# Even heads of a hybrid decoder step: ScalarE's work ordered by function table, and the queries' sums of squares ahead of the keys' product

## The reference

```python
qkv = jax.nn.silu(causal_dwconv(concat([q, k, v]), conv_prev, conv_w))
q = l2norm(split_heads(q, DN_HEADS)) * (DN_HEAD_DIM ** -0.5)   # x * rsqrt(sum(x * x) + EPS)
k = l2norm(split_heads(k, DN_HEADS))
beta = jax.nn.sigmoid(b);  G = jnp.cumsum(g, axis=-1)
decay = jnp.exp(jnp.where(causal, G[..., :, None] - G[..., None, :], -jnp.inf))
a_mat = eye + einsum('bnhid,bnhjd->bnhij', k * beta, k) * decay * strict
u_base = triangular_solve(a_mat, v * beta)
w_mat = triangular_solve(a_mat, k * beta * exp(G))
aqk = einsum('bnhid,bnhjd->bnhij', q, k) * decay
# then a scan over the chunks with q, k, G, u_base, w_mat, aqk; o is normed and multiplied by silu(z)
```

## Time and profile before

| | |
|---|---|
| median of 3 runs | 1917.39 us |
| profiled execution | 1914.43 us |
| its span, first to last instruction | 1912.6 us |
| time outside the span | 1.83 us |
| mean granted clock of TensorE | 0.978 of full |
| PE busy | 1816.6 us, 95% of the span |
| ACT busy | 619.5 us, 32% |
| POOL busy | 849.4 us, 44% |
| DVE busy | 592.2 us, 31% |
| the four even heads | about 62 to 460 us of the span |

### The profile page before, as it was taken

How to read it: one execution, slowest core, us unless ns; L and a number is a source line. 1 busy time by engine, 2 the same in 40 slices (tenths; PEclk the granted TensorE clock), 3 DMA queues, 4 the chain that set the end, 5 groups by cost and what they waited for, 6 DMA issues and landing times.

```text
span 1912.6 us, 33665 instructions
## 1 busy us (share of the span) xinstructions
PE 1816.6 (95%) x13287; PEld 1751.6 (92%) x13287; DVE 592.2 (31%) x887; ACT 619.5 (32%) x846; POOL 849.4 (44%) x1061
## 2 busy tenths in 40 slices
PE   6998999997999999999999999999988999999997
PEld 4898989886999999999999999999977999999996
DVE  2545454555211111000453355344534111111002
ACT  3625252523222222113333333424334222222112
POOL 2544444444454544446443344334424445444443
PEclk9999999997999999999999999999988999999998
DMA  5113121211222222223231343134321222322221
GB/s 149 45 34 79 43 78 44 79 34 46 66 81 82 82 79 83 80 83 103 73 117 58 114 128 112 59 117 119 106 64 58 78 87 77 88 77 83 80 83 57
DMA packets 254284, 153.23 MB, mean 80 GB/s; under 512 B 5136, under 2 KB 246549, under 8 KB 254240
## 3 DMA queue, kind: packets, MB, share of 16 engines
q1 hardware_dynamic: 239726, 140.05, 25.4%
q10 hardware_dynamic: 14514, 12.59, 2.0%
HBM read 138.26 MB, written 14.36 MB: 80 GB/s over the span
## 4 chain that ended last, share of the span: by engine, by line
PE 49%; issue 15%; POOL 10%; DVE 3%; ACT 1%; DMA 0%; POOLq 0%; ACTq 0%; DVEq 0%
PE acc L465 40%; POOL w_lo L457 9%; PE acc L485 7%; PE mx L1511 1%; DVE n_xf L587 1%; PE mx L883 1%; PE mx L528 0%; POOL n_ss L565 0%; POOL xn_lo L571 0%; DVE yT L587 0%; DMA out<-y_out 0%; DVE xn_lo L571 0%; POOL kdm L980 0%; DVE y_out L1506 0%; PE mx L524 0%
## 5 line engine op out<-in xcount | busy, mean ns | idle before, releaser
L457 POOL TENSOR_TENSOR w_lo<-raw,w_hi 128x256 fp32r<-128x256 f32 x932 | 712.7, 797 | 941.5 <-ACT w_hi L449 941.5
L465 PE MATMUL acc<-xn_hi,w_hi 128*128 128x288 f32 x2224 | 498.1, 306 | 2.4 <-ACT kb L721 1.3
L465 PE MATMUL acc<-xn_hi,w_lo 128*128 128x288 f32 x2224 | 477.6, 296 | 0.0
L465 PE MATMUL acc<-xn_lo,w_hi 128*128 128x288 f32 x2224 | 476.8, 296 | 0.0
L449 ACT ACTIVATE w_hi<-raw 128x1024 fp32r<-128x1024 f32 (+1 forms) x237 | 247.0, 1043 | 528.9 <-PE acc L465 528.2
L465 PEld LDWEIGHTS acc<-xn_hi,w_hi 128*128 128x128 f32 x2224 | 358.6, 190 | 15.7 <-issue 7.9
L465 PEld LDWEIGHTS acc<-xn_lo,w_hi 128*128 128x128 f32 x2224 | 359.2, 189 | 0.0
L465 PEld LDWEIGHTS acc<-xn_hi,w_lo 128*128 128x128 f32 x2224 | 358.9, 189 | 0.0
L601 DVE TENSOR_TENSOR x<-acc,x 128x576 f32<-128x576 f32 (+1 forms) x112 | 84.7, 756 | 323.1 <-PE acc L465 321.4
L693 DVE TENSOR_TENSOR f_h<-acc,f_g 128x576 f32<-128x576 f32 x44 | 33.3, 758 | 443.8 <-PE acc L465 443.8
L465 PE MATMUL acc<-h_hi,w_hi 128*128 128x288 f32 x704 | 150.9, 295 | 0.0
(11 more groups left out here) (326 smaller groups left out, 2134.8 us busy)
## 6 DMA issues: line engine op xcount, KB each, us to landing
raw<-in_odd_w_in SPq DMA_DIRECT2D x48, 512.0 KB, 3.7
raw<-in_ffn_w_gate SPq DMA_DIRECT2D x44, 512.0 KB, 3.7
raw<-in_ffn_w_up SPq DMA_DIRECT2D x44, 512.0 KB, 3.7
raw<-in_ffn_w_down SPq DMA_DIRECT2D x32, 512.0 KB, 3.7
raw<-in_even_w_in SPq DMA_DIRECT2D x29, 512.0 KB, 4.0
r_s<-in_state_ret SPq DMA_DIRECT2D x8, 1024.0 KB, 5.5
raw<-in_odd_w_out SPq DMA_DIRECT2D x16, 512.0 KB, 3.7
out<-r_s ACTq DMA_DIRECT2D x8, 1024.0 KB, 4.5
```

Of the source, the lines that this page charges most:

```text
L457: ins = nc.gpsimd.tensor_tensor(w_lo[:, d, piece], raw[:, s, piece], w_hi[:, d, piece].bitcast(F32), ALU.subtract)
L465: ins = nc.tensor.matmul(out, w, mv[:, tokens], start=first and n == 0, stop=last and n == 2)
```

## The change

Per head, ScalarE does the SiLU and the squares of keys and queries one after the other, and then the Ln and Exp of both. The loads of the Ln set ahead of `gr` and ahead of the Relus are gone, and so are the SiLU load and the Ln load around the queries' SiLU. One load of the Ln set stands ahead of the loop instead. With the loop's own load at L449, a head in the loop had eight loads and has four, the last head had seven and has four; with the one ahead of the loop that is 31 before and 17 now. The high split of unit 2 moves from its place between `dm` and `dt` to a place behind `dt`. The queries' inverse root is kept in `pp` (otherwise used from the second level of the inverse on) instead of `std`, so `copy_p(2)` waits for `qT`. TensorE takes `l2q` after five steps of unit 1 instead of after six steps and `kk`; the rest of unit 1 follows, and then `kk`.

```diff
-E_PE = ("rows", "l2k", "kk", "l2q", "tk", "kq", ...
+E_PE = ("rows", "l2k", "l2q", "kk", "tk", "kq", ...
-E_ACT = (..., "k_sq", "dt_lo", "dm_lo", "k_ln", "k_inv", "dm", "dt", "qs", "q_sq", "q_ln", "q_inv",
+E_ACT = (..., "k_sq", "dt_lo", "dm_lo", "qs", "q_sq", "k_ln", "k_inv", "dm", "q_ln", "q_inv", "dt",
...
             def copy_p(s):
                 e_pe.wait(act, h, f"P{s}")
+                if s == 2:
+                    e_dve.wait(act, h, "qT")
...
             ahead(split_hi, act, phase, i, 1)
-            load_table(LN_EXP)
             e_pe.wait(act, h, "rows")
...
-            load_table(LN_EXP)
             e_pool.wait(act, h, "df")
...
             evacuate_conv(act, phase, i, 0, cbuf)
+            e_dve.wait(act, h, "cq")
+            e_act.done(nc.scalar.activation(qs[:, :], cs[:, :], ACT.Silu), "qs")
+            e_act.wait(act, h, "qs")
             e_pe.wait(act, h, "l2k")
+            e_act.done(nc.scalar.activation(sq[:, :], qs[:, :], ACT.Square), "q_sq")
+            load_table(LN_EXP)
             inverse_root("k", 0, 1.0)
...
+            e_pe.wait(act, h, "l2q")
+            inverse_root("q", 2, 1.0, pp)
+            e_act.done(nc.scalar.activation(dt_[:, :], dt_[:, :], ACT.Exp, scale=-1.0), "dt")
             ahead(split_hi, act, phase, i, 2)
-            e_act.done(nc.scalar.activation(dt_[:, :], dt_[:, :], ACT.Exp, scale=-1.0), "dt")
-            load_table(SILU)
-            e_dve.wait(act, h, "cq")
...
-            load_table(LN_EXP)
-            e_pe.wait(act, h, "l2q")
-            e_dve.wait(act, h, "kT")
-            inverse_root("q", 2, 1.0)
             load_table(SILU)
...
-            U(1, 0, 6)
+            U(1, 0, 5)
+            e_act.wait(pe, h, "q_sq")
+            squares(2, "l2q")
+            U(1, 5, 8)
 
             e_dve.wait(pe, h, "kT")
             by_chunk(0, lambda c: at(kT, c), lambda c: at(kT, c))
             e_pe.done(mm(mx[0:TS, 1, 0:TS], kT[:, TP:T], kT[:, TP:T]), "kk")
-            e_act.wait(pe, h, "q_sq")
-            squares(2, "l2q")
-            U(1, 6, 8)
             e_dve.wait(pe, h, "A")
```

More of the change, by code:

```diff
@@ L218 @@
 A_DVE = ("zero", "gate", "sum", "ad", "relu", "softplus", "neg", "g", "gc0", "gc")
-E_PE = ("rows", "l2k", "kk", "l2q", "tk", "kq", "P1", "P2", "Q2", "P4", "Q4", "P8", "Q8", "tv", "P16", "Q16",
+E_PE = ("rows", "l2k", "l2q", "kk", "tk", "kq", "P1", "P2", "Q2", "P4", "Q4", "P8", "Q8", "tv", "P16", "Q16",
         "P32", "Q32", "P64", "Q64",
@@ L222 @@
         "os", "onorm", "Ss")
-E_ACT = ("gr", "eg", "ks", "k_sq", "dt_lo", "dm_lo", "k_ln", "k_inv", "dm", "dt", "qs", "q_sq", "q_ln", "q_inv",
+E_ACT = ("gr", "eg", "ks", "k_sq", "dt_lo", "dm_lo", "qs", "q_sq", "k_ln", "k_inv", "dm", "q_ln", "q_inv", "dt",
          "p2", "p4", "p8", "vs", "p16", "p32", "p64", "yah", "uu0", "uu1", "uu2", "us_", "uu3", "o_sq", "o_ln", "o_inv", "ybh")
@@ L1088, in even_scalar, with inverse_root @@
         def even_scalar(act, phase, i, h, last=False):
-            def inverse_root(name, bank, scale):
+            def inverse_root(name, bank, scale, std=std):
                 e_act.done(nc.scalar.activation(halves(std[:, :]), mx[:, bank:bank + 2, 0:HALF], ACT.Ln,
@@ L1123, in even_scalar @@
             e_act.done(nc.scalar.activation(dm[:, :], dm[:, :], ACT.Exp, scale=-1.0), "dm")
+            e_pe.wait(act, h, "l2q")
+            inverse_root("q", 2, 1.0, pp)
+            e_act.done(nc.scalar.activation(dt_[:, :], dt_[:, :], ACT.Exp, scale=-1.0), "dt")
             ahead(split_hi, act, phase, i, 2)
-            e_act.done(nc.scalar.activation(dt_[:, :], dt_[:, :], ACT.Exp, scale=-1.0), "dt")
-            load_table(SILU)
-            e_dve.wait(act, h, "cq")
-            e_act.done(nc.scalar.activation(qs[:, :], cs[:, :], ACT.Silu), "qs")
-            e_act.wait(act, h, "qs")
-            e_act.done(nc.scalar.activation(sq[:, :], qs[:, :], ACT.Square), "q_sq")
-            load_table(LN_EXP)
-            e_pe.wait(act, h, "l2q")
-            e_dve.wait(act, h, "kT")
-            inverse_root("q", 2, 1.0)
             load_table(SILU)
@@ L1325, in even_vector @@
             e_act.wait(dve, h, "q_inv")
-            step(nc.vector.scalar_tensor_tensor(out=qT[:, :], in0=qs[:, :], scalar=DN_D ** -0.5, in1=std[:, :],
+            step(nc.vector.scalar_tensor_tensor(out=qT[:, :], in0=qs[:, :], scalar=DN_D ** -0.5, in1=pp[:, :],
                                                 op0=ALU.mult, op1=ALU.mult), "qT")
```

## The result

| | before | after |
|---|---|---|
| median of eight runs each, taken side by side | 1916.93 us (1915.65 to 1919.8) | 1925.79 us (1921.33 to 1928.32) |
| ratio of after to before, 95% interval | | 1.0036 [1.0025, 1.0047] |
| profiled execution (span) | 1914.43 us (1912.6) | 1928.32 us (1926.5) |
| PE, ACT, POOL, DVE busy, us | 1816.6, 619.5, 849.4, 592.2 | 1825.1, 600.8, 851.3, 593.2 |
| mean granted clock of TensorE | 0.978 | 0.969 |

The change makes the kernel slower by 0.36%, some 7 to 9 us. ScalarE has 19 us less to do, and TensorE is busy 8.5 us longer with the same 13287 products. The profiled execution of after is the longest of its eight, so medians, not the two profiles, carry the size.

The account below looks back on a forecast made before the run. TensorE's waits for `q_sq` and `kd` were taken as one chain, set by late ScalarE. Forecast: 1914.43 + 0.4 contention + 6.0 clock = 1920.8, plus 1.0 toward the runs' median = 1921.8 us; range 1914 to 1926.

Parts of the forecast that it names:

- The first wait goes: TensorE's wait for the queries' squares `q_sq` ahead of `l2q` disappears, 1.86 us of it in the second head.
- 1.4 us earlier: How much earlier than before `kq` on TensorE would be out of the way, ending at 184.65.
- The table loads are worth nothing by themselves: Fourteen fewer loads save 18.0 us of ScalarE's time, but were costed at nothing for the kernel's time.
- GpSimd's masked `dt` becomes the limit and `P1` stays where it was: Low split starts 182.85, `dtm` ends 187.13, `P1` stays at 189.13; TensorE waits 4.5 us in one piece.
- Contention: VectorE's `qT` meeting GpSimd's low split of unit 2: 0.1 us a head, 0.4 in all.
- The bound of 0.5 for a stretched split: Upper end for `qT` and low split overlapping: 0.5 us a head if one waits for the other.
- The clock: Behind the 4.5 us wait, TensorE runs at half pace after `P1`: 1.5 us a head, 6.0 in all.
- My upper end, 1.6: Highest clock loss a head allowed behind `P1`, half of a 3.2 us slow stretch.
- From one execution to the runs: Profiled execution was 2.96 us below the runs' median; 1.0 of it was added to the forecast.
- Sum: On the profiled execution 1914.43 + 0.4 + 6.0 = 1920.8; with 1.0 carried to the runs, 1921.8 us.
- No change that can be measured: Rival, chance 0.37: same chain, but clock loss behind `P1` small or equally paid before; 1917.8 us on the runs' scale.
- Faster, by a chain that GpSimd does not set: Rival, chance 0.15: masked `dt` ready by `kq`'s end, `P1` 2.4 us a head earlier; -9.5, 1908 on the runs' scale.

Follow-up runs that it names:

- e5_loads_back: Changed kernel with two ScalarE table loads put back into each even head, at its start and ahead of the Relus: 1925.77 us, ratio 1.0039 to before.
- e1_mask_first: Changed kernel with GpSimd making masked `dt` and first mask `b1` ahead of the low split of unit 2: 1942.32 us, ratio 1.0131 to before.
- e2_split_early: Changed kernel with ScalarE's high split of unit 2 moved into its idle time ahead of `cq`: 1936.28 us, ratio 1.0091 to before.
- e3_filler: Changed kernel with 15 idle products on TensorE between `kq` and `P1` in each even head: 1915.93 us, ratio 0.9996 to before.
- e13_guard_early: Changed kernel, high split of unit 2 ahead of `cq`; GpSimd waits for `cq` before the low split, `qT` before the mask: 1908.09 us, ratio 0.9957.
- e10_before_filler: Kernel before the change with 15 idle products on TensorE between `kq` and `P1`: 1918.75 us, ratio 1.0008 to before.
- e15_guard_early_fill: e13_guard_early with 7 idle products in TensorE's 2.15 us wait ahead of `P1`: 1905.21 us, ratio 0.9923 to the kernel before.
- e6_z_first: Changed kernel with VectorE's `z1` ahead of the small `xi`: 1924.46 us, ratio 1.0028 to before.

## Why the prediction was right, point by point

*The first wait goes.* Right: no wait for `q_sq` in the list, and `kq` ends early. The "1.4 us earlier" of the prediction is 2.4 by its own numbers (184.65 against 185.62 + 1.42), and 2.2 in the trace; nothing in the sum hangs on it.

*The table loads are worth nothing by themselves.* Right, shown for eight of the 14 by e5_loads_back.

*GpSimd's masked `dt` becomes the limit and `P1` stays where it was.* Right in place and size. The chain was forecast on the clock of the old head; with the 2.23 us of its later start taken off, the low split starts at 182.90 (forecast 182.85), `dtm` ends at 187.52 (187.13), and `P1` starts at 189.51 (189.13). The wait is 4.65 us (4.5). From `cq` to `P1` it is 14.41 us, within the 0.5 us of 14.0 that I named.

*Contention.* The term was 0.1 a head, 0.4 in all; `P1` moved by 0.5 in all. In the second head the split takes 3.13 us beside `qT`, where it took 2.78, and that 0.35 is nearly the whole of the 0.38 by which `P1` moves there. The bound of 0.5 for a stretched split held. But I treated this as a small term of one sign; e1_mask_first and e2_split_early show that the same meeting costs 3.7 to 6.5 us of `qT` when GpSimd is already at work as `qT` starts; the 1.44 us of the earlier trace rows was a small sign of it. That after does not pay it is an accident of its order that the prediction did not name.

*The clock.* The mechanism was right and this is the mis-sized term: 1.5 a head, 6.0 in all, against 1.96 a head by e3_filler, 7.8 in all. I took the 3.0 us at half pace behind the wait of 3.21 us; behind 4.65 us the stretch lasted about 5 us. My upper end, 1.6, came from the slow stretch of before and was too low as well. The rule of the Trainium skill that the prediction weighed (TensorE: Matmul & The Clock Gate, section HAM oscillation) is borne out in its direction: e3_filler keeps the array at work through the same gap, and the loss is gone.

*From one execution to the runs.* I carried 1.0 of the 2.96 us by which the profiled execution lay under the median, on the guess that ordinary runs of before pay for the clock behind `kd`. No run shows that. Slower runs of before do have a lower mean clock (in e13_guard_early's rounds 1912.29 us at 0.979 and 1922.14 at 0.975), but not where they lose it: e3_filler, with that wait filled, spreads as far (1912.88 to 1924.74), and e10_before_filler pays for its own products. Carrying all 2.96 would have given 1923.8, nearer to the 1925.79 measured, so the term moved the forecast the wrong way.

*Sum.* 0.5 for `P1` and 7.8 for the clock are 8.3 us, and the medians differ by 8.9. The forecast had 4.4 on the scale of the runs: right in sign, half of the size. Of what it lacked, the clock is 1.8 and the part of the 2.96 that was not carried 2.0. 1925.79 lies inside the range by 0.2 us, and that is luck in part: the clock passed its upper end (1.96 a head against 1.6), and the end of the range held only because `P1` moved by 0.5 in all and not by the 2.0 that the end allows.

*The rivals.* "No change that can be measured" needed the clock to hold, which e3_filler shows to be the very thing that failed. "Faster, by a chain that GpSimd does not set" was not what this change does, and its price of 2.4 us a head was sound once `qT` is guarded: e13_guard_early and e15_guard_early_fill move `P1` by 2.1 us against before.

## What to carry to other kernels

When a change removes one of two waits, follow the second one back to its own engine: two short waits joined into one long one can cost more than they did apart, because TensorE came out of it at half clock here, and a few idle products in the wait are a cheap test of that. Before an idle engine is given earlier work, look at what its idleness protects: here GpSimd's wait kept VectorE's `qT` short, and a wait of GpSimd on that operation was worth more than having the work early. And when work is put later, name its next user too.

## What the runs showed of the hardware that was not expected

*A VectorE operation held by GpSimd.* `qT`, 128x576 with both sources in SBUF, takes 0.76 us alone, 4.49 us in e2_split_early and 7.21 us in e1_mask_first, beside GpSimd operations that follow one another; a 64x64 `xi` took 3.46 us, though the same `xi` beside the same split took 0.70 us in the second head of after. Operations with a source in PSUM, such as `aqk` (0.69), kept their length beside the same work. The Trainium skill (GPSIMD Engine Reference, section Specifications) lists the SBUF interfaces as shared between the two engines, with contention for VectorE's instructions with two SBUF inputs. The trace agrees and adds the size, which that section does not give: in e1_mask_first the time of several GpSimd operations. There and in e2_split_early `qT` ends 0.65 and 0.67 us behind the start of unit 3's split, and that split takes 3.29 us where it took 2.78 before, which looks like a stop and then a turn of its own, not like a slower pace. In the other direction, the split that started 0.26 us behind `qT` in after took 3.13 us instead of 2.78: it lost 0.35 of the 0.50 us in which both ran. What finally lets the held operation through was not tried.

*The clock does not go by the length of the last wait.* Behind a wait of 2.09 us before kept 1.00, and behind 2.15 us e13_guard_early fell to 0.50 in the same head. Nor does the code ahead settle it: behind the same wait of 1.86 us for `q_sq`, with the same code in that head up to there, the stretch from 181.80 to 185.00 was at 0.52 in before and at 1.00 in e10_before_filler. Behind the waits of 3.47 to 4.67 us ahead of `P1`, all twelve heads in the traces of after, e5_loads_back and e6_z_first had the slow stretch (`P2` 4.04 to 5.92 us behind `P1`). What decides at about 2 us these runs leave open.
